# The gate table of the first layer: who builds its one-hot matrices

## The chip, the cores and the metric

The kernel runs on one core of a Trainium2 chip. The metric is the device time of one execution, in microseconds (us), as the median of several runs. Its engines are called as in the profile: PE (TensorE, with PEld for its weight loads), DVE (VectorE), ACT (ScalarE), POOL (GpSimd), SP (SyncE, which only issues DMAs here).

## What is computed

Two layers of token mixing (four head groups) and of a product-key expert network, PEER, on 256 latent and 256 context tokens. The part that matters here is the expert network of the first layer. Each token has 8 heads; each head picks 16 of 128 x 128 experts, and a gate for each:

```
best, sel = lax.top_k(cand, PEER_TOPK)
eidx = jnp.take_along_axis(cidx, sel, axis=-1)     # i * 128 + j
g = jax.nn.softmax(best, axis=-1)
act = jax.nn.gelu(jnp.einsum('td,thkd->thk', xb, u[eidx]))
return jnp.einsum('thk,thkd->td', (g * act), v[eidx])
```

So a token has 8 x 16 = 128 picks (i, j, gate). For the 256 latent tokens of the first layer the kernel does not gather rows of u and v. It runs all 16384 experts as dense matrix products and multiplies their activations by a table of gates G[j, i, token], which is zero wherever an expert was not picked. This table is what the changed stage builds.

## The kernel before

`phase_route` finds the picks and leaves three matrices iT, jT, gT, each 128 x 256: one column for each latent token, one partition for each of its 128 picks. `phase_dense` turns them into the table, `phase_mixed` uses it. `phase_dense` is called once, in the first layer. Each phase is a block of its own: all engines meet at a barrier before and after it, so no load of `phase_mixed` is issued while `phase_dense` runs, and the block ends only when its last store has landed.

For one token the table is one matrix product of two one-hot matrices, 128 picks x 128 keys each. `hot_j` holds 1 where the key equals j, `hot_i` holds the gate where the key equals i. PE multiplies them and leaves the token's 128 x 128 gates in PSUM.

The 256 tokens go through in 16 units of U = 16 tokens. `hot_i` and `hot_j` have two buffers each (r = unit mod 2), and so has PSUM (four of its eight banks per unit). For unit u:

- DVE (L1746) makes columns 0 to UJ - 1 of `hot_j`, UJ = 10 tokens, in a single comparison of `jT` and `iota`, both read from SBUF and broadcast: 128 x 1280 elements.
- DVE (L1750) then makes all 16 matrices of `hot_i`, one instruction each: 128 x 128 elements of `iota`, compared with the pointer scalar iT[:, token] and multiplied by the pointer scalar gT[:, token].
- ACT makes the other 6 tokens of `hot_j`: |iota - j| for each (L1783), then one relu(1 - x) over all six (L1786).
- PE (L1771) waits for all three (semaphores a, b, c), and for the PSUM buffer, and does 16 products. Each is in float32 and shows as two rows of the trace, so a unit is 32.
- ACT (L1800) copies the unit's PSUM, 128 x 2048, into `dense_stage`. ACT makes its columns of unit u + 1 before it copies unit u.
- SP (L1812) stores four units at once, 4 MB, to HBM.
- POOL has no work in this phase.

Before unit u, DVE waits until PE has done unit u - 2, which frees the buffer (`dve.wait_ge(g_mm, u - 1)`). The first eight units are written out, the other eight are the body of a register loop `Fori(1, 2)`, which runs once.

Of the kernel before, what the change touches and what calls it, by code (L numbers as in the profile page):

```python
# [33 lines left out]
ALU = mybir.AluOpType  # L34
ACT = mybir.ActivationFunctionType
AX = mybir.AxisListType.X

P = 128
# [46 lines left out]
NKEY = 128  # L85
TOPK = 16
GROWS = 4
TB = 64
# [34 lines left out]
def bc(ap, axis, n):  # L123

    ap = ap.unsqueeze(axis)
    shape = list(ap.shape)
    shape[axis] = n
    return ap.to_broadcast(shape)
# [13 lines left out]
def build(nc, d, out):  # L142
# [4 lines left out]
    def sem(name):  # L147
        layer_sems.append(nc.alloc_semaphore(name=name))
        return layer_sems[-1]
# [7 lines left out]
    def sb(st, name, shape, dt=F32):  # L157
        return st.enter_context(nc.sbuf_tensor(name, shape, dt))

    with ctx:  # L160
        ps = ctx.enter_context(nc.psum_tensor("ps", [P, 8, BANK], F32))
# [11 lines left out]
        iota = sb(ctx, "iota", [P, P])  # L173
        gates_dram = nc.dram_tensor("peer_gates", (T // TB, P, NKEY, TB), F32, kind="Internal").ap()
# [13 lines left out]
        class AdaPart:  # L188
# [53 lines left out]
            def columns(self, pe, i):  # L242

                pe.wait_ge(ada_row_ev, self.chunks0 + i + 1)
                for j in range(4):
                    o = 2 * (4 * i + j)
                    mm = nc.tensor.matmul(ps[:, self.banks[2], o:o + 2], self.row[:, i % 2, j * P:(j + 1) * P], sel[:],
                                          start=True, stop=True)
                mm.then_inc(ada_col_mm, 1)
# [1471 lines left out]
        def phase_dense(l, lo, iT, jT, gT):  # L1721


            n = T - lo
            U = 16
            UB = 8
            PB = TB // U
            UJ = 10
            a_done, b_done, g_mm, g_ev, neg_done, dist_done, c_done = (
                sem(f"dense_{x}{l}") for x in ("a", "b", "mm", "ev", "neg", "dist", "c"))  # L1730
            stored = [sem(f"dense_stored{l}_{r}") for r in range(2)]
            with ExitStack() as st:
                hot_i = sb(st, f"hot_i{l}", [P, 2, U, NKEY])
                hot_j = sb(st, f"hot_j{l}", [P, 2, U, NKEY])
                stage = sb(st, f"dense_stage{l}", [P, 2, NKEY, TB])
                njT = sb(st, f"dense_nj{l}", [P, n + U])
                with nc.Block() as block:
                    @block.vector
                    def _(dve):
                        def body(it, first):  # L1740
                            for q in range(UB):
                                u = UB * it + q
                                r = q % 2
                                if not (first and q < 2):
                                    dve.wait_ge(g_mm, u - 1)
                                nc.vector.tensor_tensor(hot_j[:, r, 0:UJ], bc(jT[:, bass.ds(u * U, UJ)], 2, NKEY),  # L1746
                                                        bc(iota[:], 1, UJ), ALU.is_equal).then_inc(b_done, 1)
                                for t in range(U):
                                    at = bass.ds(u * U + t, 1)
                                    last = nc.vector.tensor_scalar(hot_i[:, r, t], iota[:], iT[:, at], gT[:, at],  # L1750
                                                                   ALU.is_equal, ALU.mult)
                                last.then_inc(a_done, 1)
                        nc.vector.memset(njT[:, n:], 0.0).then_inc(neg_done, 1)
                        nc.vector.tensor_scalar(njT[:, 0:n], jT[:], -1.0, None, ALU.mult).then_inc(neg_done, 1)
                        body(0, True)
                        with dve.Fori(1, n // (U * UB)) as it:
                            body(it, False)

                    @block.tensor
                    def _(pe):  # L1760
                        def body(it, first):
                            for q in range(UB):
                                u = UB * it + q
                                r = q % 2
                                pe.wait_ge(b_done, u + 1)
                                pe.wait_ge(a_done, u + 1)
                                pe.wait_ge(c_done, u + 1)
                                if not (first and q < 2):
                                    pe.wait_ge(g_ev, u - 1)
                                for t in range(U):  # L1770
                                    mm = nc.tensor.matmul(ps[:, 4 * r + t // 4, (t % 4) * P:(t % 4 + 1) * P],  # L1771
                                                          hot_j[:, r, t], hot_i[:, r, t], start=True, stop=True)
                                mm.then_inc(g_mm, 1)
                        body(0, True)
                        with pe.Fori(1, n // (U * UB)) as it:
                            body(it, False)

                    @block.scalar
                    def _(act):
                        def columns(u, r):  # L1780

                            for t in range(UJ, U):
                                last = nc.scalar.activation(hot_j[:, r, t], iota[:], ACT.Abs, bias=njT[:, bass.ds(u * U + t, 1)])  # L1783
                            last.then_inc(dist_done, 1)
                            act.wait_ge(dist_done, u + 1)
                            nc.scalar.activation(hot_j[:, r, UJ:], hot_j[:, r, UJ:], ACT.Relu, scale=-1.0,  # L1786
                                                 bias=onecol[:]).then_inc(c_done, 1)

                        def body(it, first):
                            for q in range(UB):  # L1790
                                u = UB * it + q
                                if not (first and q == 0):
                                    act.wait_ge(g_mm, u)
                                columns(u + 1, (q + 1) % 2)
                                act.wait_ge(g_mm, u + 1)
                                if q % PB == 0 and not first:
                                    act.wait_ge(stored[q // PB], 16 * it)
                                got = ps[:, 4 * (q % 2):4 * (q % 2) + 4, :].rearrange("p b (t i) -> p i (b t)", i=NKEY)
                                o = (q % PB) * U
                                nc.scalar.activation(stage[:, q // PB, :, o:o + U], got, ACT.Copy).then_inc(g_ev, 1)  # L1800
                        act.wait_ge(neg_done, 2)
                        columns(0, 0)
                        body(0, True)
                        with act.Fori(1, n // (U * UB)) as it:
                            body(it, False)

                    @block.sync
                    def _(sp):
                        with sp.Fori(0, n // (U * UB)) as it:
                            for r in range(2):  # L1810
                                sp.wait_ge(g_ev, UB * it + PB * r + PB)
                                sp.dma_start(gates_dram[bass.ds(2 * it + r, 1)].rearrange("a p i t -> p (a i) t"),  # L1812
                                             stage[:, r]).then_inc(stored[r], 16)
                        for r in range(2):
                            sp.wait_ge(stored[r], 16 * (n // (U * UB)))


        def phase_stream(l, lo, hp, hT, q):
# [594 lines left out]
        for l in range(DEPTH):  # L2413
# [16 lines left out]
            with ExitStack() as st:  # L2430
# [3 lines left out]
                if last_layer:  # L2434
                    hp = [(CTX, T, *own)]
                    clear_layer_sems()
                    q = QueryWeights(st, l)
# [4 lines left out]
                else:  # L2442
                    eid, eidT = (sb(st, f"{x}{l}", [P, nt, PH * TOPK], U32) for x in ("eid", "eidT"))
                    gate = sb(st, f"gate{l}", [P, nt, PH * TOPK])
                    with ExitStack() as st1:
                        iT, jT, gT = (sb(st1, f"{x}T{l}", [P, T - CTX]) for x in "ijg")
                        with ExitStack() as st2:
                            hp = [(0, CTX, *(sb(st2, f"h2c_{x}{l}", [P, DC, CTX], F32R) for x in ("hi", "lo"))), (CTX, T, *own)]
                            q = QueryWeights(st2, l)
# [8 lines left out]
        with ExitStack() as st:  # L2458
            y = sb(st, "y", [P, DC, T])
            phase_norm("norm_final", d["final_norm_g"], None, None, CTX, y)  # L2460
            stored = sem("stored")
# [107 lines left out]
```

## Time and profile before

| | |
|---|---|
| median of 3 runs | 3184.79 us (3181.0 to 3188.43) |
| the profiled execution | 3183.49 us, its span 3181.7 us |
| busy, of the span | PE 80%, DVE 64%, ACT 34%, POOL 35% |
| `phase_dense`, DVE's first `hot_j` to the end of its last `hot_i` | 872.27 to 961.43 us, 89.2 us |
| mean granted TensorE clock | 0.888 of full speed |

A row of the timeline gives the start in us, the time from the first start to the last end, the engine, the line of the kernel, the operation, what it writes and reads, the shape, and how many instructions it merges; brackets give the idle time before and what ended it. Instructions of one engine overlap a little: the next starts before the last one's end, so the pace of a series is read from start to start. The columns of the other views stand with their rows below.

### The profile page before, as it was taken

Reading aid. Unit: us, or ns where it says so; the run is one execution under the profiler, and the core shown is the slowest. Engines: PE = TensorE matmul, PEld = TensorE weight load, DVE = VectorE, ACT = ScalarE, POOL = GpSimd, SP = SyncE. Lnnn points to the kernel's source line nnn. Section 1 sums busy time; section 2 is a strip of 40 time slices with the busy share of each in tenths; the row PEclk is TensorE's granted clock in tenths of the full one; section 3 lists DMA queues with packets and bytes.
Section 4 is the critical chain, followed back from the end, with each engine's and each line's share of the span. In section 5 each row is a group of like instructions: output and inputs, shape, how many; then the busy total and the mean of one; then the engine's idle time right before and its main releaser. Section 6 shows DMA issues by size and latency. Waiting matters only on the chain. (4 is left out here: it accounts for less than half of the span.)

```text
span 3181.7 us, 41584 instructions
## 1 busy us (share of the span) xinstructions
PE 2546.1 (80%) x15562; PEld 1903.4 (60%) x15562; DVE 2022.4 (64%) x4495; ACT 1084.4 (34%) x2179; POOL 1119.1 (35%) x1013
## 2 busy tenths in 40 slices
PE   5978699797376778878799999888877797777776
PEld 3778445595165777767777777577746553222222
DVE  3566435489995989887844333467543699845444
ACT  3422235321073333333333333342234443333332
POOL 1024100331005667556665555212302354433431
PEclk8985589897698989999999999988678899999999
DMA  5210141135238999999999999621002799999996
GB/s 208 74 30 1 62 159 42 53 113 180 106 152 325 405 407 404 363 401 385 402 406 406 405 406 406 263 87 43 9 1 85 303 391 422 421 421 422 421 422 258
DMA packets 211897, 816.93 MB, mean 257 GB/s; under 512 B 22681, under 2 KB 41689, under 8 KB 178033
## 3 DMA queue, kind: packets, MB, share of 16 engines
q0 software_dynamic: 110592, 536.92, 41.7%
q1 hardware_dynamic: 101104, 277.35, 23.4%
q8 instruction: 124, 2.03, 0.3%
q14 instruction: 77, 0.62, 0.1%
HBM read 796.37 MB, written 17.83 MB: 256 GB/s over the span
## 5 line engine op out<-in xcount | busy, mean ns | idle before, releaser
L1919 PE MATMUL ps<-pair_ring,pair_diag 128*128 128x512 f32 x1024 | 476.3, 610 | 144.8 <-ACT pair_diag L1993 142.2
L2103 DVE CUSTOM_DVE_ANT_0 pair_ring<-pair_ring,hT 128x1024 f32<-128x1024 f32 x256 | 312.9, 1222 | 206.7 <-DMA pair_ring<-in_uv_rows,eid 206.7
L1919 PEld LDWEIGHTS ps<-pair_ring,pair_diag 128*128 128x128 f32 x1024 | 187.1, 192 | 423.3 <-ACT pair_diag L1993 228.5
L1883 POOL DMA_INDIRECT pair_ring<-in_uv_rows,eid x256 | 268.2, 1048 | 391.9 <-PE ps L1919 364.0
L2251 POOL DMA_INDIRECT sparse_ring<-in_v_rows,eidT x256 | 279.5, 1092 | 298.4 <-PE ps L2300 226.9
L2251 POOL DMA_INDIRECT sparse_ring<-in_u_rows,eid x256 | 339.4, 1326 | 122.5 <-issue 68.1
L118 PE MATMUL ps<-h_hi,peer_uh 128*128 128x256 f32 x1024 | 310.1, 303 | 85.6 <-DVE peer_ul L2363 77.9
L2389 DVE CUSTOM_DVE_ANT_0 sparse_ring<-sparse_ring,hT 128x1024 f32<-128x1024 f32 x256 | 304.7, 1224 | 41.9 <-DMA sparse_ring<-in_u_rows,eid 35.7
L120 PE MATMUL ps<-h_hi,peer_ul 128*128 128x256 f32 x1024 | 299.2, 292 | 1.1 <-issue 0.9
L119 PE MATMUL ps<-h_lo,peer_uh 128*128 128x256 f32 x1024 | 299.4, 292 | 0.1
L118 PEld LDWEIGHTS ps<-h_hi,peer_uh 128*128 128x128 f32 x1024 | 206.0, 201 | 149.4 <-DVE peer_ul L2363 92.0
L118 PE MATMUL ps<-peer_wh,peer_vh 128*128 128x256 f32 x1024 | 291.3, 285 | 1.8 <-issue 1.7
L119 PE MATMUL ps<-peer_wl,peer_vh 128*128 128x256 f32 x1024 | 290.5, 284 | 0.4 <-issue 0.3
L120 PE MATMUL ps<-peer_wh,peer_vl 128*128 128x256 f32 x1024 | 290.1, 283 | 0.1
L2363 DVE TENSOR_TENSOR peer_ul<-peer_u,peer_uh 128x1024 fp32r<-128x1024 f32 x128 | 156.5, 1223 | 164.3 <-ACT peer_uh L2328 132.7
L2328 ACT ACTIVATE peer_uh<-peer_u 128x1024 fp32r<-128x1024 f32 x128 | 135.2, 1057 | 292.2 <-DMA peer_u<-in_uT 273.7
L120 PEld LDWEIGHTS ps<-h_hi,peer_ul 128*128 128x128 f32 x1024 | 206.2, 201 | 1.3 <-issue 1.3
L119 PEld LDWEIGHTS ps<-h_lo,peer_uh 128*128 128x128 f32 x1024 | 206.6, 202 | 0.2 <-issue 0.2
L118 PEld LDWEIGHTS ps<-peer_wh,peer_vh 128*128 128x128 f32 x1024 | 197.8, 193 | 2.6 <-issue 2.4
L119 PEld LDWEIGHTS ps<-peer_wl,peer_vh 128*128 128x128 f32 x1024 | 197.5, 193 | 2.1 <-issue 2.1
L120 PEld LDWEIGHTS ps<-peer_wh,peer_vl 128*128 128x128 f32 x1024 | 197.2, 193 | 0.8 <-issue 0.8
L2300 PE MATMUL ps<-sparse_ring,sparse_wdiag 128*32 128x512 f32 x1024 | 137.2, 653 | 67.2 <-DMA sparse_ring<-in_v_rows,eidT 66.2
(397 smaller groups left out, 5411.5 us busy)
## 6 DMA issues: line engine op xcount, KB each, us to landing
peer_u<-in_uT SPq DMA_DIRECT2D x128, 512.0 KB
peer_v<-in_v_rows SPq DMA_DIRECT2D x128, 512.0 KB
ada_slab<-in_ada_w SPq DMA_DIRECT2D x20, 2048.0 KB, 8.6
proj_slab<-in_w_fm SPq DMA_DIRECT2D x38, 512.0 KB
route_slab<-in_w_pq SPq DMA_DIRECT2D x32, 512.0 KB, 3.3
peer_gates<-dense_stage SPq DMA_DIRECT2D x4, 4096.0 KB, 13.1
peer_gates<-peer_gates SPq DMA_DIRECT2D x32, 512.0 KB
out_slab<-in_w_out SPq DMA_DIRECT2D x16, 512.0 KB, 3.7
```

What stands on the lines that cost most here:

```text
L118: nc.tensor.matmul(out, w[0], x[0], start=start, stop=False)
L119: nc.tensor.matmul(out, w[0], x[1], start=False, stop=False)
L120: return nc.tensor.matmul(out, w[1], x[0], start=False, stop=stop)
L1883: nc.gpsimd.indirect_dma_start(out=ring[:, s % R], out_offset=None, in_=d["uv_rows"], in_offset=bass.IndirectOffsetOnAxis(ap=eid[:, s:s + ...
L1919: mm = nc.tensor.matmul(ps[:, 4 + 2 * t + half, :], diag[:, s % DG, :], ring[:, s % R, D_MODEL + half * BANK:D_MODEL + (half + 1) * BANK], ...
L2103: nc.vector.tensor_tensor_reduce(out=row, in0=row, in1=hT[:, s // NS], scale=1.0, scalar=0.0, op0=ALU.mult, op1=ALU.add, accum_out=dots[:, ...
L2251: nc.gpsimd.indirect_dma_start(out=ring[:, s % R], out_offset=None, in_=rows, in_offset=bass.IndirectOffsetOnAxis(ap=at, axis=0)).then_inc ...
L2300: mm = nc.tensor.matmul(ps[32 * q:32 * (q + 1), 6 + half, :], wdiag[:, q, j, :], ring[:, s % R, half * BANK:(half + 1) * BANK], start=(j = ...
L2328: nc.scalar.activation(uh[:, e % 2], us[:, e % SW], ACT.Copy).then_inc(uhi, 1)
L2363: nc.vector.tensor_tensor(ul[:, e % 2], us[:, e % SW], f32(uh[:, e % 2]), ALU.subtract).then_inc(ulo, 1)
L2389: nc.vector.tensor_tensor_reduce(out=ring[:, s % R], in0=ring[:, s % R], in1=hT[:, t], scale=1.0, scalar=0.0, op0=ALU.mult, op1=ALU.add, a ...
```

## The change

Three things change in `phase_dense`, and nothing elsewhere:

1. `hot_i`: DVE makes the first UI = 10 of a unit's 16 matrices, POOL the last 6, by the same instruction (`nc.gpsimd.tensor_scalar`). POOL waits for the buffer as DVE does, and signals a semaphore of its own, `a_pool`, for which PE waits too.
2. `hot_j`: UJ goes from 10 to 12. DVE's comparison has 128 x 1536 elements; ACT makes four columns and not six.
3. The register loops of all engines are written out as 16 units.

```
-            UJ = 10
+            UJ = 12
+            UI = 10
...
+                        for u in range(NU16):
+                            r = u % 2
+                            if u >= 2:
+                                dve.wait_ge(g_mm, u - 1)
+                            nc.vector.tensor_tensor(hot_j[:, r, 0:UJ], bc(jT[:, u * U:u * U + UJ], 2, NKEY),
+                                                    bc(iota[:], 1, UJ), ALU.is_equal).then_inc(b_done, 1)
+                            for t in range(UI):
+                                at = slice(u * U + t, u * U + t + 1)
+                                last = nc.vector.tensor_scalar(hot_i[:, r, t], iota[:], iT[:, at], gT[:, at], ALU.is_equal, ALU.mult)
+                            last.then_inc(a_done, 1)
+
+                    @block.gpsimd
+                    def _(pool):
+                        for u in range(NU16):
+                            r = u % 2
+                            if u >= 2:
+                                pool.wait_ge(g_mm, u - 1)
+                            for t in range(UI, U):
+                                at = slice(u * U + t, u * U + t + 1)
+                                last = nc.gpsimd.tensor_scalar(hot_i[:, r, t], iota[:], iT[:, at], gT[:, at], ALU.is_equal, ALU.mult)
+                            last.then_inc(a_pool, 1)
...
+                            pe.wait_ge(b_done, u + 1)
+                            pe.wait_ge(a_done, u + 1)
+                            pe.wait_ge(a_pool, u + 1)
+                            pe.wait_ge(c_done, u + 1)
```

The order of DVE's instructions, from the start of the phase through unit 1 to the first wait for a buffer (`dense_mm0` is the semaphore g_mm). Before:

```order
L1754 TENSOR_SCALAR dense_nj<-jT 128x256
L1746 TENSOR_TENSOR hot_j<-jT,iota 128x1280
L1750 TENSOR_SCALAR hot_i<-iota,iT,gT 128x128 x16
L1746 TENSOR_TENSOR hot_j<-jT,iota 128x1280
L1750 TENSOR_SCALAR hot_i<-iota,iT,gT 128x128 x16
L1746 TENSOR_TENSOR hot_j<-jT,iota 128x1280 [waits dense_mm0]
```

In the changed kernel:

```order
L1743 TENSOR_SCALAR dense_nj<-jT 128x256
L1748 TENSOR_TENSOR hot_j<-jT,iota 128x1536
L1752 TENSOR_SCALAR hot_i<-iota,iT,gT 128x128 x10
L1748 TENSOR_TENSOR hot_j<-jT,iota 128x1536
L1752 TENSOR_SCALAR hot_i<-iota,iT,gT 128x128 x10
L1748 TENSOR_TENSOR hot_j<-jT,iota 128x1536 [waits dense_mm0]
```

Six instructions of a unit have left DVE's queue, and the comparison is wider; the wait stands at the same place.

The order of POOL's instructions at the same place, as a piece of the difference (the rows without a sign are in both). POOL goes from the routing phase into the new work; units 0 and 1 wait for nothing, and are the first twelve:

```order
 L1638 TENSOR_TENSOR route_wl<-route_slab,route_wh 128x1024 [waits query_hi0] x14
 L1541 UNCONDITIONAL_BRANCH
+L1755 UNCONDITIONAL_BRANCH [waits barrier_Pool_Activation_PE_DVE_SP_gather]
+L1763 TENSOR_SCALAR hot_i<-iota,iT,gT 128x128 x12
+L1763 TENSOR_SCALAR hot_i<-iota,iT,gT 128x128 [waits dense_mm0]
+L1763 TENSOR_SCALAR hot_i<-iota,iT,gT 128x128 x5
```

The last two rows repeat for each of units 2 to 15. Where POOL had nothing, it now has 96 instructions in the phase, and PE waits for each sixth.

## Rows read from the trace of the kernel before

**Rows 1.** Timeline of DVE from 922.5 us, in the middle of the phase.

```profile
922.80 1.48 DVE L1746 TENSOR_TENSOR hot_j<-jT,iota 128x1280 f32<-128x1280 f32 x1
924.20 4.19 DVE L1750 TENSOR_SCALAR hot_i<-iota,iT,gT 128x128 f32<-128x128 f32 x16
928.31 1.48 DVE L1746 TENSOR_TENSOR hot_j<-jT,iota 128x1280 f32<-128x1280 f32 x1
```

**Rows 2.** Timelines of PE and of ACT in the same stretch.

```profile
922.99 3.81 PE L1771 MATMUL ps<-hot_i,hot_j 128*128 128x128 f32 x32 [1.69 <-issue]
...
923.10 1.85 ACT L1783 ACTIVATE hot_j<-iota,dense_nj 128x128 f32<-128x128 f32 x6
924.99 0.93 ACT L1786 ACTIVATE hot_j<-hot_j,onecol 128x768 f32<-128x768 f32 x1
926.83 1.88 ACT L1800 ACTIVATE dense_stage<-ps 128x2048 f32<-128x2048 f32 x1 [0.91 <-PE ps L1771]
```

**Rows 3.** Timeline of all engines, start and end of the phase.

```profile
872.27 1.49 DVE L1746 TENSOR_TENSOR hot_j<-jT,iota 128x1280 f32<-128x1280 f32 x1
...
877.96 7.28 PE L1771 MATMUL ps<-hot_i,hot_j 128*128 128x128 f32 x42 [7.14 <-ACT hot_j L1786]
...
884.17 1.49 DVE L1746 TENSOR_TENSOR hot_j<-jT,iota 128x1280 f32<-128x1280 f32 x1 [0.80 <-PE ps L1771]
...
957.24 4.18 DVE L1750 TENSOR_SCALAR hot_i<-iota,iT,gT 128x128 f32<-128x128 f32 x16
...
965.36 1.88 ACT L1800 ACTIVATE dense_stage<-ps 128x2048 f32<-128x2048 f32 x1 [0.91 <-PE ps L1771]
980.25 0.34 SPq L2229 DMA_DIRECT2D peer_u<-in_uT  x1
```

**Rows 4.** Single lines: count, duration in ns (min/median/max), first and last start.

```profile
L1783 ACT ACTIVATE hot_j<-iota,dense_nj x102: 385/390/401, 872.4 to 963.1; 128x128 f32<-128x128 f32 x102
...
L2363 DVE TENSOR_TENSOR peer_ul<-peer_u,peer_uh x128: 1209/1224/1300, 985.9 to 2015.1; 128x1024 fp32r<-128x1024 f32 x128
```

**Rows 5.** Busy us by stretch (PE, PEld, DVE, ACT, POOL), then granted PE clock.

```profile
878.00:884.00 6.00, 6.00 (x33) 6.00 (x34) 5.37 (x17) 0.00 (x0) 0.00 (x0) 0.59 0.00 0
```

**Rows 6.** Lines of POOL as in rows 4; the last has count, busy us, mean ns.

```profile
L630 POOL TENSOR_SCALAR mix<-mix,mod x12: 1012/1064/1599, 47.7 to 2075.9; 128x256 f32<-128x256 f32 x12
...
L811 POOL TENSOR_TENSOR scan_exk<-cum x28: 393/590/791, 236.2 to 2262.4; 128x256 f32<-128x256 f32 x14, 128x128 f32<-128x128 f32 x14
...
L630 POOL TENSOR_SCALAR mix<-mix,mod 128x256 f32<-128x256 f32 x12 | 13.9, 1171 | 92.2 <-ACT h_hi L597 92.2
```

**Rows 7.** Timelines of POOL and of DVE around 52 to 55 us.

```profile
51.59 2.11 POOL L630 TENSOR_SCALAR mix<-mix,mod 128x256 f32<-128x256 f32 x2
...
52.44 1.09 DVE L734 SCALAR_TENSOR_TENSOR mix<-xT,norm_mix_amp,proj_tslab 128x256 f32<-128x256 f32 x2
...
55.26 0.87 DVE L719 SCALAR_TENSOR_TENSOR h_lo<-mix,mod,h_hi 128x256 fp32r<-128x256 f32 x2
```

**Rows 8.** Timelines of DVE and of POOL from 631 us.

```profile
631.11 0.28 DVE L440 CAST h2c_hi<-h 128x256 fp32r<-128x256 f32 x1
631.31 0.83 DVE L440 CAST h_hi<-h 128x256 fp32r<-128x256 f32 x1
...
631.26 0.73 POOL L457 TENSOR_TENSOR h2c_lo<-h,h2c_hi 128x256 fp32r<-128x256 f32 x1 [0.76 <-DVE h_hi L440]
```

**Rows 9.** Timelines of POOL and of DVE from 224 us.

```profile
224.13 3.96 POOL L807 TENSOR_TENSOR scan_exq<-cum 128x256 f32<-128x256 f32 x1 [13.09 <-DVE scan_lk L857]
228.05 0.61 POOL L808 TENSOR_TENSOR scan_exk<-cum 128x256 f32<-128x256 f32 x1
...
226.92 0.68 DVE L870 TENSOR_TENSOR mix<-fm 128x512 f32<-128x512 f32 x1
```

**Rows 10.** Single lines of DVE, one and two pointer scalars, columns as in rows 4.

```profile
L1323 DVE TENSOR_SCALAR diag<-ident,rinv x48: 285/286/290, 423.4 to 2400.7; 128x128 f32<-128x128 f32 x48
...
L1325 DVE TENSOR_SCALAR diag<-ident,rinv,nlam x24: 345/346/348, 482.9 to 2401.5; 128x128 f32<-128x128 f32 x24
```

More of the change, by code:

```diff
@@ L1727, in phase_dense @@
             PB = TB // U
-            UJ = 10
-            a_done, b_done, g_mm, g_ev, neg_done, dist_done, c_done = (
-                sem(f"dense_{x}{l}") for x in ("a", "b", "mm", "ev", "neg", "dist", "c"))
+            UJ = 12
+            UI = 10
+            NU16 = n // U
+            a_done, a_pool, b_done, g_mm, g_ev, neg_done, dist_done, c_done = (
+                sem(f"dense_{x}{l}") for x in ("a", "a_pool", "b", "mm", "ev", "neg", "dist", "c"))
             stored = [sem(f"dense_stored{l}_{r}") for r in range(2)]
@@ L1739, in _ @@
                     def _(dve):
[L1740 to L1752, printed above, removed]
@@ L1753, in _ @@
                         nc.vector.memset(njT[:, n:], 0.0).then_inc(neg_done, 1)
                         nc.vector.tensor_scalar(njT[:, 0:n], jT[:], -1.0, None, ALU.mult).then_inc(neg_done, 1)
-                        body(0, True)
-                        with dve.Fori(1, n // (U * UB)) as it:
-                            body(it, False)
+                        for u in range(NU16):
[8 more added lines that the diff above has]
+                            last.then_inc(a_done, 1)
@@ L1759, in _ @@
                     @block.tensor
                     def _(pe):
[L1761 to L1773, printed above, removed]
@@ L1774, in _ @@
-                        body(0, True)
-                        with pe.Fori(1, n // (U * UB)) as it:
-                            body(it, False)
+                        for u in range(NU16):
+                            r = u % 2
+                            pe.wait_ge(b_done, u + 1)
+                            pe.wait_ge(a_done, u + 1)
+                            pe.wait_ge(a_pool, u + 1)
+                            pe.wait_ge(c_done, u + 1)
+                            if u >= 2:
+                                pe.wait_ge(g_ev, u - 1)
+                            for t in range(U):
+                                mm = nc.tensor.matmul(ps[:, 4 * r + t // 4, (t % 4) * P:(t % 4 + 1) * P],
+                                                      hot_j[:, r, t], hot_i[:, r, t], start=True, stop=True)
+                            mm.then_inc(g_mm, 1)
@@ L1778, in _, with columns @@
                     @block.scalar
                     def _(act):
-                        def columns(u, r):
+                        def columns(u):
+                            r = u % 2
                             for t in range(UJ, U):
-                                last = nc.scalar.activation(hot_j[:, r, t], iota[:], ACT.Abs, bias=njT[:, bass.ds(u * U + t, 1)])
+                                last = nc.scalar.activation(hot_j[:, r, t], iota[:], ACT.Abs, bias=njT[:, u * U + t:u * U + t + 1])
@@ L1787, in columns @@
                                                  bias=onecol[:]).then_inc(c_done, 1)
[L1789 to L1792, printed above, removed]
-                                    act.wait_ge(g_mm, u)
[L1794 to L1805, printed above, removed]
+                        act.wait_ge(neg_done, 2)
+                        columns(0)
+                        for u in range(NU16):
+                            if u + 1 < NU16:
+                                if u >= 1:
+                                    act.wait_ge(g_mm, u)
+                                columns(u + 1)
+                            act.wait_ge(g_mm, u + 1)
+                            b = u // PB
+                            if u % PB == 0 and b >= 2:
+                                act.wait_ge(stored[b % 2], 16 * (b // 2))
+                            got = ps[:, 4 * (u % 2):4 * (u % 2) + 4, :].rearrange("p b (t i) -> p i (b t)", i=NKEY)
+                            o = (u % PB) * U
+                            nc.scalar.activation(stage[:, b % 2, :, o:o + U], got, ACT.Copy).then_inc(g_ev, 1)
@@ L1807, in _ @@
                     @block.sync
                     def _(sp):
[L1809 to L1813, printed above, removed]
+                        for b in range(n // TB):
+                            sp.wait_ge(g_ev, PB * (b + 1))
+                            sp.dma_start(gates_dram[b:b + 1].rearrange("a p i t -> p (a i) t"), stage[:, b % 2]).then_inc(stored[b % 2], 16)
@@ L1814, in _ @@
                         for r in range(2):
-                            sp.wait_ge(stored[r], 16 * (n // (U * UB)))
+                            sp.wait_ge(stored[r], 16 * (n // TB // 2))
         def phase_stream(l, lo, hp, hT, q):
```

## The prediction

> **What bounds the kernel now.** The change touches one stage of 3%, so I read that stage and not the shares of the span. I took the timeline of the middle of the phase first, engine by engine. DVE has no gap: a unit begins at 922.80 and the next at 928.31, so a unit costs 5.51 us [rows 1]. 1.40 us of it is the comparison (from its start to the start of what follows), 4.11 us the sixteen `hot_i`, 0.257 us each. PE works 3.81 us of a unit and idles 1.69; ACT is busy 1.85 + 0.93 + 1.88 = 4.66 us [rows 2]. The waits say the same: DVE waits for PE once, 0.80 us before unit 2 [rows 3], while ACT waits 0.91 us for PE in each unit [rows 2]. DVE is the bound, and PE's idle time is time in which it waits for DVE.
>
> Next I asked whether the stage's time reaches the end of the kernel. The last copy to the stage buffer ends at 967.24, and the first load of the next phase is issued at 980.25, after the store has landed and the engines have met [rows 3]. Nothing of the next phase starts early, so each microsecond that the last unit moves goes whole to the end. From DVE's first comparison to the end of its last `hot_i` it is 961.42 - 872.27 = 89.2 us [rows 3]: sixteen units of 5.51 and 1 us of wait and start. This is the number that the change moves.
>
> **The change, part by part.**
>
> *DVE.* It loses six `hot_i`: 6 x 0.257 = 1.54 us of a unit. Its comparison grows from 1280 to 1536 elements. 1280 take 1.48 us [rows 1], 1024 take 1.22 [rows 4], so 256 more cost 0.26. A unit of DVE becomes 5.51 - 1.54 + 0.26 = 4.23 us, if nothing disturbs it.
>
> *ACT.* It loses two |iota - j| of six (1.85 us) and a third of the relu. Four cost some 1.26 us; the relu over 512 columns lies between 0.39 us at 128 [rows 4] and 0.93 at 768 [rows 2], in proportion 0.72. With the copy ACT has 3.86 us. ACT was not the bound at 4.66 and is not now; this move costs or gives something only through DVE's 0.26.
>
> *PE.* Same products, one more wait. 3.81 us at full clock. At the start it is slower: the first unit's products run from 877.96 until they release DVE at 884.17, 6.2 us [rows 3], with a granted clock of 0.59 [rows 5], between the levels 1.2 and 2.4 GHz; PE had idled before. That binds only where a unit is under 6.2 us.
>
> *The loops.* The loop body ran once, so writing it out removes a branch or two on each engine. DVE's `hot_i` have the same pace in the first eight units and in the loop: 16 in 4.19 us at 924.20 and in 4.18 at 957.24 [rows 1, 3]. I cost it at nothing.
>
> *POOL.* This is the term that decides. Six instructions of 128 x 128 with two pointer scalars and two operations; the trace has none. Nearest is L630, the same kind, with one pointer scalar and 256 columns: median 1064 ns, and a pair takes 2.11 us, 1.055 each [rows 6, 7]. How much of that goes with the columns? While such an instruction runs, a pair of DVE's takes 1.09 us instead of 0.87 [rows 7]: DVE is held 0.22 us, for 256 columns. I take that as the part that goes with the columns, and the rest of the 1.06 us as a fixed part, during which DVE runs on. Half the columns save 0.11: 0.945 us. The second pointer scalar costs 0.06 us on DVE (346 against 286 ns) [rows 10], and I put as much on POOL: **1.0 us**. Bounds: below, the fastest two-tensor instruction of POOL at 128 columns, 0.39 us; above, the mean of the twelve of L630, 1.17 us [rows 6], with 0.06 for the pointer 1.23. I stay near L630 as it is the same kind of instruction. Six then take 6.0 us (2.4 to 7.4). The point from which POOL decides is low: 5.51 / 6 = 0.92 us each.
>
> The Trainium skill ("GPSIMD Engine Reference", 4.1 Engine selection) says of elementwise work on GpSimd that one-input operations are roughly at line rate. By that (an estimate from its 1.2 GHz clock: 128 columns in 0.11 us, and a dispatch) POOL would be hidden, and the sum would be that of the faster rival below. The row of 1064 ns for 256 columns [rows 6] speaks against it, and I go by the row.
>
> *POOL against DVE.* The two disturb each other, in both directions. A cast of DVE, 0.28 us alone, takes 0.83 when it starts 0.05 us after an instruction of POOL [rows 8]. And POOL's instruction at 224.13 takes 3.96 us instead of 0.61: it finishes only 0.5 us after the last of a burst of DVE's two-input instructions, the one that ends at 227.60 [rows 9]. So DVE's wide comparison (two inputs, 1.66 us here) can hold POOL once a unit by 0 to 1.66 us. A fixed part of an instruction of POOL can pass meanwhile; half of that part is 0.4 us, and less is lost for some phases of the two, so I take 0.9. In return POOL holds DVE by 6 x 0.11 = 0.66 us a unit: DVE's 4.23 become 4.9.
>
> *Sum.* DVE 4.9, ACT 3.9, PE 3.8, POOL 6.0 + 0.9 = 6.9 us. With two buffers POOL works back to back, since PE's unit is done 3.9 us after POOL's and the next-but-one buffer is free by then. PE waits for `a_pool` in every unit, and DVE, done early, waits for PE. Sixteen units of 6.9 are 110.4 us in place of 89.2: +21.2. The profiled execution has 3183.49 us, so 3204.7; the median of the runs shown is 1.3 above it. **Forecast: 3206 us.** This case's own range: units of 5.9 to 7.4 + 1.66 = 9.0 us, +5 to +55, that is 3190 to 3240.
>
> **The rivals.**
>
> *Faster: DVE stays the bound.* If POOL's instruction costs 0.39 to 0.65 us, POOL's six and one hold stay below DVE's 4.9. Then 16 x 4.9 = 78.4 us, and the first two units of PE at the low clock add 2 x (6.2 - 4.9) = 2.6: 81.0, or 8 us less than now, 3177 us. If the holds come to nothing too, 16 x 4.23 and 3.9 for the two units are 71.6: 17.6 less, 3167. For it: 590 ns is the median of POOL's two-tensor instructions [rows 6]. Against: L630 never took less than 1012.
>
> *No change: a draw.* POOL's instruction at 0.70 to 0.83 us, or holds that rarely meet, give units of 5.2 to 5.9 us: within 6.4 us of now, 3185. It would mean that L630's fixed part is shorter without DVE beside it. That the written-out loops are all that counts would end here too.
>
> *Much slower: the two exclude each other whole.* If a running instruction of POOL holds DVE for its full length, as in [rows 8], and DVE holds POOL for all of its own, a unit is 4.23 + 6.0 = 10.2 us: 164 in place of 89.2, +74, 3259 us. The 0.22 us of [rows 7] speaks against it for this kind of instruction. The Trainium skill ("SBUF — State Buffer", Who interferes with whom) says that VectorE and GpSimd share a pair of ports, and that whoever issues first gets the shared pair "for the whole instruction"; by that rule this rival would be the forecast, at 3259 us; [rows 7] show less.
>
> **How the numbers follow.** A change under 0.2% (6.4 us) can't be told from none in this kernel. POOL as the bound 0.57; DVE as the bound 0.22; the draw 0.16; exclusion 0.05. That gives faster 0.22, same 0.16, slower 0.62. The sign hangs on one price, POOL's instruction: 0.92 us with no hold at all, about 0.8 with the hold that I expect. The range goes from 3174 to 3240: up to the upper bound of the forecast's case, down into the faster one; it leaves out exclusion, and the part of the faster rival with hardly any holds (0.08).
>
> **What would show it.** Right: L1763 on POOL at about 1 us with no gap between units, one of six longer; DVE's `hot_j` (L1748) waiting for PE by some 2 us in each unit; PE's wait for `hot_i` of L1763; unit starts 6.9 us apart. DVE's `hot_i` above 0.257 us in pace shows the holds. The forecast is wrong if POOL idles before its first instruction of each unit, waiting for PE: then its six fit, and DVE or PE sets the pace. Outside this phase all stages should keep their times.

## The result, and the profile after

The changed kernel takes **3208.71 us** (median of 4 runs, 3203.66 to 3210.25), in place of 3184.05 with the runs of before repeated beside it: a ratio of 1.0072, 95% interval 1.0058 to 1.0086. It is slower, by about 25 us; the forecast was 3206.

| | before | after |
|---|---|---|
| span of the profiled execution | 3181.7 us | 3207.2 us |
| DVE's first `hot_j` | 872.27 | 873.50 |
| first `hot_j` to the end of the last `hot_i` of either engine | 89.1 us | 111.3 us |
| first load of the next phase | 980.25 | 1003.82 |
| one unit, later part of the phase | 5.51 us | 6.88 us |
| POOL, instructions and busy time in the phase | none | 96, 104.5 us |

The phase gives 22.1 us of the 25.5 between the two spans. 1.2 us were there when it began, and some 2 us came after it; both lie in code that the change doesn't touch, and the runs of one kernel differ by more (from 3203.66 to 3210.25 here).

Timelines of the changed kernel, each of one engine, in the middle of the phase: DVE, then PE, then POOL (cut at different places, so the counts go with the cut).

```profile
921.14 1.75 DVE L1748 TENSOR_TENSOR hot_j<-jT,iota 128x1536 f32<-128x1536 f32 x1
922.81 2.80 DVE L1752 TENSOR_SCALAR hot_i<-iota,iT,gT 128x128 f32<-128x128 f32 x10
930.66 1.76 DVE L1748 TENSOR_TENSOR hot_j<-jT,iota 128x1536 f32<-128x1536 f32 x1 [5.05 <-PE ps L1777]
...
935.01 1.74 DVE L1748 TENSOR_TENSOR hot_j<-jT,iota 128x1536 f32<-128x1536 f32 x1
...
925.28 8.92 PE L1777 MATMUL ps<-hot_i,hot_j 128*128 128x128 f32 x64 [4.95 <-POOL hot_i L1763]
...
930.73 2.45 POOL L1763 TENSOR_SCALAR hot_i<-iota,iT,gT 128x128 f32<-128x128 f32 x1 [0.97 <-PE ps L1777]
...
934.84 2.42 POOL L1763 TENSOR_SCALAR hot_i<-iota,iT,gT 128x128 f32<-128x128 f32 x1
...
939.74 3.88 POOL L1763 TENSOR_SCALAR hot_i<-iota,iT,gT 128x128 f32<-128x128 f32 x5
944.50 2.45 POOL L1763 TENSOR_SCALAR hot_i<-iota,iT,gT 128x128 f32<-128x128 f32 x1 [0.88 <-PE ps L1777]
```

Beside [rows 1, 2], DVE has lost its place as the bound: it works in pairs of units, two comparisons 4.35 us apart, and then waits 5.05 us for PE. PE waits 4.95 us for POOL, and does two units in one go. POOL is busy from 930.73 to 943.62 and idle for 0.88 us: 12 of its instructions in 13.77 us, two units. At the end of a pair, with DVE idle, five in a row take 3.88 us, a pace of 0.773 us. Two of the twelve take much longer, and both meet a comparison. The first of the pair takes 2.45 us: it starts 0.07 us after DVE's comparison, and ends 0.8 us after the comparison has given way to the `hot_i`. The fourth starts at 934.84, 0.17 us before the second comparison, and takes 2.42 us; the comparison takes its 1.74 us all the same. I call this lengthening the hold.

The waits of the whole phase (total, times, longest):

```profile
PE ps L1777 <- POOL hot_i L1763: 44.5, 8, 9.9
DVE hot_j L1748 <- PE ps L1777: 36.6, 7, 6.2
...
POOL hot_i L1763 <- PE ps L1777: 8.1, 7, 2.1
```

Lines of the changed kernel (count, ns min/median/max), and two stretches (busy us of PE, PEld, DVE, ACT, POOL, then the granted clock):

```profile
L1748 DVE TENSOR_TENSOR hot_j<-jT,iota x16: 1744/1746/1759, 873.5 to 976.2; 128x1536 f32<-128x1536 f32 x16
...
L1752 DVE TENSOR_SCALAR hot_i<-iota,iT,gT x160: 330/386/430, 875.2 to 980.3; 128x128 f32<-128x128 f32 x160
...
L1763 POOL TENSOR_SCALAR hot_i<-iota,iT,gT x96: 783/834/2497, 873.3 to 984.0; 128x128 f32<-128x128 f32 x96
...
925.30:930.60 5.30, 5.30 (x34) 5.30 (x35) 0.32 (x2) 0.00 (x0) 4.46 (x6) 0.70 0.00 0
930.70:939.00 8.30, 3.50 (x32) 3.31 (x30) 8.30 (x21) 7.37 (x12) 8.27 (x7) 0.99 0.30 126
```

The first unit of a pair is multiplied after PE has idled for 5 us, with a granted clock of 0.70 between the levels 1.2 and 2.4 GHz, and takes 5.4 us (925.28 to 930.66) where 3.8 would do. This is what POOL then waits for: the first unit of the next pair needs this one's buffer. POOL's own work on a pair is done before that: in the next pair at 943.62, where PE's first unit is done at 944.43.

### The profile page after: what moved, and what is told of

The parts are those of the page before. It is cut to its first block and busy times, and to the rows that moved or that the text cites. A ratio compares the mean times of both kernels' runs of the same rounds, so it can differ in the third digit from the quotient of the medians.

```text
span 3207.2 us, 41519 instructions
## 1 busy us (share of the span) xinstructions
PE 2549.8 (80%) x15562; PEld 1907.5 (59%) x15562; DVE 2003.9 (62%) x4399; ACT 1067.8 (33%) x2140; POOL 1232.3 (38%) x1109
## 5 line engine op out<-in xcount | busy, mean ns | idle before, releaser
L2249 POOL DMA_INDIRECT sparse_ring<-in_u_rows,eid x256 | 346.5, 1354 | 119.3 <-issue 68.1
```

The costliest lines, as they stand in the source:

```text
L2249: nc.gpsimd.indirect_dma_start(out=ring[:, s % R], out_offset=None, in_=rows, in_offset=bass.IndirectOffsetOnAxis(ap=at, axis=0)).then_inc ...
```

## The experiments

Three things could carry the 22 us: the price of POOL's instruction, the hold by DVE's comparison, and the clock. The experiments take them apart. In the ratios "before" is the kernel before, run beside them; the phase is measured as in the table above, in the one execution that was profiled, while the times are medians of 4 to 11 runs.

**The loops alone.**

```
-            UI = 10
+            UI = 16
-            UJ = 12
+            UJ = 10
...
-                            pe.wait_ge(a_pool, u + 1)
```

with POOL's block taken out.

> Only the loops are written out: UJ = 10, all sixteen hot_i on VectorE, none on GpSimd. My theory (all of the 25 us comes from GpSimd's part): units of 5.51 us as before, the phase from the first hot_j to the end of the last hot_i 89.2 us, the time within 6 us of before, 3184. Rival (the straight code costs something of its own, in fetching): units longer than 5.51, the time up to 10 us above before.

3183.52 us, ratio 0.9998 (0.9985 to 1.0011), phase 88.8 us. DVE's timeline in it:

```profile
922.08 1.47 DVE L1748 TENSOR_TENSOR hot_j<-jT,iota 128x1280 f32<-128x1280 f32 x1
923.49 4.18 DVE L1752 TENSOR_SCALAR hot_i<-iota,iT,gT 128x128 f32<-128x128 f32 x16
927.59 1.47 DVE L1748 TENSOR_TENSOR hot_j<-jT,iota 128x1280 f32<-128x1280 f32 x1
```

A unit of 5.51 us, as in [rows 1]. The loops are worth nothing here.

**The two columns back on ACT.** `-UJ = 12`, `+UJ = 10` in the changed kernel.

> As the changed kernel, with the two columns of hot_j back on ScalarE (UJ = 10). Theory (VectorE's two-input comparison holds GpSimd for its whole length, once a unit, and GpSimd is the bound): a comparison shorter by 0.26 us shortens every unit by 0.26 us, 6.88 to 6.62, the phase 111.3 to about 107 us, the time about 4 us under the changed kernel, 3204. Rival (VectorE has slack, so its 0.26 us is hidden; the hold does not go with the comparison's length): the phase stays at 111 us, the time at 3208.

3205.48 us, ratio 1.0053 (1.0036 to 1.0069), phase 109.2 us: 2.1 us less than the changed kernel, half of what I expected. (The ratios of the two, 1.0053 and 1.0072, have intervals that overlap, so it is the phase that tells them apart.) Its waits:

```profile
PE ps L1777 <- POOL hot_i L1763: 40.3, 8, 9.4
DVE hot_j L1748 <- PE ps L1777: 38.8, 7, 6.3
...
POOL hot_i L1763 <- PE ps L1777: 10.2, 7, 2.2
```

The longest instruction of POOL fell from 2497 to 2232 ns, and its busy time by 3.9 us (104.5 to 100.6), as the hold's theory says. But POOL's wait for PE grew from 8.1 to 10.2 us: half of the gain went there. Moving the columns to DVE was a small loss of its own, through the hold and not through DVE's time.

**No two-input comparison.**

```
-                            nc.vector.tensor_tensor(hot_j[:, r, 0:UJ], bc(jT[:, u * U:u * U + UJ], 2, NKEY),
-                                                    bc(iota[:], 1, UJ), ALU.is_equal).then_inc(b_done, 1)
+                            for t in range(UJ):
+                                at = slice(u * U + t, u * U + t + 1)
+                                last = nc.vector.tensor_scalar(hot_j[:, r, t], iota[:], jT[:, at], None, ALU.is_equal)
+                            last.then_inc(b_done, 1)
```

> As the changed kernel, but VectorE makes its twelve columns of hot_j with twelve one-input instructions with a pointer scalar, instead of one comparison of two inputs. VectorE gets more work: 12 x 0.20 = 2.4 us in place of 1.67. Theory (the comparison holds GpSimd): without it GpSimd's six cost about 0.83 to 0.85 us each, 5.1 us, VectorE needs 2.4 + 2.57 + 0.3 = 5.3 us, a unit is 5.3 to 5.5 us and the phase about 87 us: the time 3182, 26 us under the changed kernel. Rival (the long first instruction of GpSimd in each unit has another cause, such as starting after a wait): the phase stays at 111 us or above, the time 3208 or more.

3180.92 us, ratio 0.9987 (0.9977 to 0.9998), phase 86.2 us. DVE got more work, and the phase became 25.1 us shorter. Its lines, PE's longest wait for DVE or POOL, and a stretch:

```profile
L1750 DVE TENSOR_SCALAR hot_j<-iota,jT x192: 269/275/393, 871.0 to 954.0; 128x128 f32<-128x128 f32 x192
...
L1765 POOL TENSOR_SCALAR hot_i<-iota,iT,gT x96: 834/845/1156, 870.8 to 956.3; 128x128 f32<-128x128 f32 x96
...
PE ps L1779 <- DVE hot_i L1754: 26.7, 14, 7.0
...
900.00:940.00 40.00, 29.13 (x248) 27.97 (x246) 40.00 (x166) 27.42 (x45) 40.00 (x46) 1.00 0.50 211
```

No instruction of POOL is above 1.16 us now, and the one that PE sees come last is DVE's. POOL has no gap either, so the two are level. DVE does not stop POOL with its one-input instructions, but it delays it: the 96 have a mean of 0.90 us, from 0.84 beside the `hot_i` to as much as 1.16 beside the `hot_j`, in place of the 0.79 of POOL alone. The 25.1 us are not the hold's alone: the pairs are gone too, and the clock is granted in full, so this run takes away the hold and POOL's wait for a slow PE together. That these instructions of DVE disturb POOL far less than the comparison is measured; which port each of them uses is not.

**TensorE kept busy.**

```
+                            if u >= 2:
+                                pe.wait_ge(g_ev, u - 1)
+                                for t in range(8):
+                                    nc.tensor.matmul(ps[:, 4 * r, 0:P], ident[:], ident[:], start=True, stop=True)
                             pe.wait_ge(b_done, u + 1)
...
                             pe.wait_ge(c_done, u + 1)
-                            if u >= 2:
-                                pe.wait_ge(g_ev, u - 1)
```

> As the changed kernel, with eight products of the identity by itself before each unit from the third on, into the PSUM bank that the unit then overwrites; TensorE waits for that bank first and for the one-hots after. Theory (in every second unit the products run at the lower clock after 5 us of idling, 5.4 us instead of 3.8, and GpSimd then waits 0.97 us for their end): with the clock kept up GpSimd does not wait, the phase falls from 111.3 to about 103.5 us, the time to 3201. Rival (that wait is not the clock's): the phase stays at 111 us, or grows where the filler gets in the way of the second of two units.

3203.2 us, ratio 1.0053 (1.0036 to 1.007), phase 105.3 us: 6.0 us less than the changed kernel, 7.8 expected. A stretch of it, the same stretch of the changed kernel, and POOL's wait in the filler run:

```profile
900.00:964.00 64.00, 55.72 (x480) 54.11 (x479) 45.85 (x114) 38.36 (x64) 64.00 (x61) 1.00 0.43 182
```

```profile
900.00:964.00 64.00, 41.90 (x308) 41.06 (x306) 41.14 (x100) 35.45 (x57) 58.79 (x54) 0.88 0.31 132
```

```profile
POOL hot_i L1763 <- PE ps L1779: 2.9, 2, 1.8
```

The clock is granted in full, POOL has no gap in the 64 us, and from the seventh unit on DVE's comparisons come evenly, 6.4 us apart: 6 x 0.80 and one hold of 1.6. The first units still came in pairs, which is probably most of what is missing.

**GpSimd's price.** In the changed kernel, POOL only compares (for six of sixteen tokens the gate is left out):

```
-                                last = nc.gpsimd.tensor_scalar(hot_i[:, r, t], iota[:], iT[:, at], gT[:, at], ALU.is_equal, ALU.mult)
+                                last = nc.gpsimd.tensor_scalar(hot_i[:, r, t], iota[:], iT[:, at], None, ALU.is_equal)
```

> As the changed kernel, but GpSimd's instructions only compare: one pointer scalar and one operation. It leaves out the multiplication by the gate for six of sixteen tokens. Undisturbed they took 0.773 us with two. If the forecast's reading of the nearest row was right but for the second pointer's price (0.06 us), they now take about 0.71 us, and the 1.05 us of 256 columns means 0.34 us for 128 columns more. If the fixed part is smaller and the columns cost more than the 0.11 us read from VectorE's delay, the same 0.34 us shows it, or more where the second scalar is dear: at 0.60 us, 0.45. A unit should shorten by six times the difference, 0.4 us at 0.71 (the phase by 6 us) and 1.0 us at 0.60 (16 us).

3201.32 us, ratio 1.0045 (1.0028 to 1.0061), phase 103.1 us. POOL's line and timeline, PE's and DVE's rows for the second half of a pair, and two stretches:

```profile
L1763 POOL TENSOR_SCALAR hot_i<-iota,iT x96: 591/597/2188, 872.9 to 975.6; 128x128 f32<-128x128 f32 x96
```

```profile
925.16 10.11 POOL L1763 TENSOR_SCALAR hot_i<-iota,iT 128x128 f32<-128x128 f32 x12 [3.49 <-PE ps L1777]
...
927.31 2.33 POOL L1763 TENSOR_SCALAR hot_i<-iota,iT 128x128 f32<-128x128 f32 x4
...
938.79 10.11 POOL L1763 TENSOR_SCALAR hot_i<-iota,iT 128x128 f32<-128x128 f32 x12 [3.52 <-PE ps L1777]
...
932.02 10.24 PE L1777 MATMUL ps<-hot_i,hot_j 128*128 128x128 f32 x64 [3.38 <-POOL hot_i L1763]
...
938.73 1.76 DVE L1748 TENSOR_TENSOR hot_j<-jT,iota 128x1536 f32<-128x1536 f32 x1 [4.51 <-PE ps L1777]
```

```profile
924.50:930.00 5.50, 4.14 (x38) 3.95 (x36) 4.89 (x12) 4.86 (x7) 4.83 (x6) 1.00 0.00 0
...
935.00:939.00 4.00, 4.00 (x25) 4.00 (x25) 0.27 (x1) 0.27 (x1) 0.48 (x2) 0.62 1.22 518
```

Four in 2.33 us with a last one of 0.597 are a pace of 0.578 us, so the second scalar and the second operation cost 0.195 us. L630, with one scalar and 256 columns, never took under 1012 ns [rows 6], these never under 591: by that 128 columns are worth 0.42 us, an estimate, since L630 adds where these compare. The time is where the expectation failed: 12 instructions fell from 12.9 to 10.1 us, and a pair of units still takes 13.63 (925.16 to 938.79) after 13.77. POOL idles 3.5 us of it, waiting for the first unit of the pair on PE, which runs from 932.02 to 938.73 at the low clock. The bound had moved to PE, whose granted clock is low after it has idled for 3.4 us.

**The same, with TensorE kept busy** (four products of the identity before each unit):

> The last kernel (GpSimd only compares; it leaves out the gate for six of sixteen tokens) with four products of the identity before each unit from the third on, as in the filler run, where they were eight. There GpSimd's price had fallen by a quarter and two units still took 13.6 us, with a granted clock of 0.62 while the first of the two was multiplied. Theory (TensorE's clock after its idle time is what holds the pace there): with TensorE kept busy a unit costs what GpSimd costs, 6 x 0.577 + 1.6 = 5.1 us, the phase falls from 103 to 83 to 86 us and the time by 17 to 20 us, to 3183. Rival (the pace of pairs comes from the buffers and the comparisons, not from the clock): 6.5 us or more a unit, the phase at 100 us or above.

3188.79 us, ratio 1.0014 (1.0003 to 1.0024), phase 86.5 us, 16.6 us less than without the filler. Stretch and POOL's timeline:

```profile
900.00:930.00 30.00, 25.19 (x221) 24.90 (x222) 24.95 (x61) 20.82 (x35) 27.96 (x34) 1.00 0.58 245
```

```profile
927.05 8.40 POOL L1763 TENSOR_SCALAR hot_i<-iota,iT 128x128 f32<-128x128 f32 x9 [0.68 <-PE ps L1779]
```

A pair takes 10.8 us, 5.4 a unit, where 5.1 were expected. Both holds of a pair fall into its first unit; POOL's six of the second are then done in 3.5 us, before PE's 3.8 at full clock are, and POOL waits 0.68 us a pair. So the clock was the bound of the run before: four useless products a unit took 16.6 us off its phase. The times moved less, by 12.5 us, or some 10 by the two ratios, and this one lies above before although its phase is the shorter one. The profiled execution took 3183.7 us, 5 under the median; what the rest is, no run shows.

**Other shares.** The prices say that four on POOL fit. Three runs in the changed kernel with other UI and UJ.

> As the changed kernel, with UI = 12 and UJ = 10: GpSimd makes four of sixteen, ScalarE keeps its six columns. By the prices measured so far: GpSimd 4 x 0.82 + a hold of 1.35 = 4.6 us a unit, VectorE 1.40 + 12 x 0.257 + 4 x 0.05 = 4.7, ScalarE 4.5 to 4.7, TensorE 3.8 and slower in the first units. Units of 4.7 us, the phase 77 to 80 us in place of 89.2: the time 3174 to 3177, about 10 us under before. Rival (with VectorE, ScalarE and GpSimd within 0.2 us of each other, waits between them add up): units of 5.0 us or more, the gain under 6 us.

> As the one before, with UI = 13: GpSimd makes three. GpSimd 3 x 0.82 + 1.35 = 3.8 us and idle, VectorE 1.40 + 13 x 0.257 + 3 x 0.05 = 4.9 us and the bound: units of 4.9 us, the phase 79 to 82 us, the time 3176 to 3179. If waits between the engines are what costs at UI = 12, this one is the faster of the two; if not, it is slower by 0.2 us a unit, 3 us.

> As UI = 12, with UJ = 11: one column goes from ScalarE to VectorE. ScalarE falls to 4.2 us, VectorE rises to 4.8, GpSimd's hold to 1.48 and its unit to 4.8. If VectorE and GpSimd set the pace, units of 4.8 us and the time 2 us above UJ = 10; rival (at UJ = 10 ScalarE's 4.5 to 4.7 us is what binds): faster than UJ = 10 or the same.

| UI, UJ | median | ratio (95%) | phase | unit |
|---|---|---|---|---|
| 12, 10 | 3172.97 us | 0.9962 (0.9948 to 0.9976) | 76.6 us | 4.64 us |
| 13, 10 | 3177.59 us | 0.9978 (0.9970 to 0.9987) | 78.9 us | 4.83 us |
| 12, 11 | 3173.69 us | 0.9963 (0.9950 to 0.9976) | 78.5 us | 4.78 us |

The phases order the three as the prices do; the medians can't tell 12, 10 from 12, 11. The timeline of the first, and a stretch of it:

```profile
921.72 1.48 DVE L1748 TENSOR_TENSOR hot_j<-jT,iota 128x1280 f32<-128x1280 f32 x1
...
922.02 3.81 PE L1777 MATMUL ps<-hot_i,hot_j 128*128 128x128 f32 x32 [0.83 <-DVE hot_i L1752]
...
923.12 3.41 DVE L1752 TENSOR_SCALAR hot_i<-iota,iT,gT 128x128 f32<-128x128 f32 x12
...
926.36 1.48 DVE L1748 TENSOR_TENSOR hot_j<-jT,iota 128x1280 f32<-128x1280 f32 x1
...
900.00:940.00 40.00, 33.11 (x280) 31.63 (x278) 40.00 (x115) 39.27 (x72) 40.00 (x36) 1.00 0.56 237
```

DVE has no gap, PE idles 0.83 us and keeps its clock. POOL has no gap either, so its four have no room left. With UI = 12 and UJ = 10 the kernel is 12 us faster than before and 36 faster than the changed one, by two numbers: the hold and the price are there still, but four of sixteen just fit beside DVE's twelve.

## Why the prediction was right, and which terms were off

**The forecast's case came.** POOL became the bound, PE waits for its semaphore, the phase grew by 22.1 us (21.2 in the sum), and 6.88 us a unit stand where 6.9 were forecast. That the two agree so closely is luck: three terms were mis-sized, and they cancel.

- *POOL's instruction, 1.0 us.* Measured 0.773 alone and 0.83 beside DVE's `hot_i`. The step that failed is "I take that as the part that goes with the columns": DVE's delay of 0.22 us was read as the cost of 256 columns to POOL, so halving them saved only 0.11. By the run without the gates they save about 0.42. The second pointer scalar, with the second operation, costs 0.20 and not DVE's 0.06. Six: 4.8 us, not 6.0.
- *The hold, 0.9 us.* Measured 1.6 a unit, nearly the whole length of the comparison (2.45 us in place of 0.83). "Half of that part is 0.4 us, and less is lost for some phases" assumed that the fixed part of POOL's instruction could pass under the comparison; it doesn't. [rows 9] had shown it: there POOL finished only after the last instruction of the burst.
- *"With two buffers POOL works back to back, since PE's unit is done 3.9 us after POOL's ..."* The first unit of a pair is done 5.4 us after, since PE has idled and its clock is low. 0.9 to 1.0 us of idling a pair of units, 8.1 us in the phase. The forecast's sum had nothing for this: the prediction saw the low clock at the start alone, where it "binds only where a unit is under 6.2 us".
- With the sizes measured, a unit is six instructions, one hold and half of a pair's idling: 6 x 0.80 + 1.6 + 0.48 = 6.9 us, where the forecast had 6.0 + 0.9 + 0.

**What held.** DVE's comparison has 1746 ns (1.74 = 1.48 + 0.26 predicted). POOL's holds on DVE were put at 0.11 each, and are some 0.05: ten `hot_i` and the comparison take 4.35 us with two or three of them in place of 4.23. ACT needs 1.26 + 0.72 + 1.88, as forecast. The loops cost nothing. Nothing outside the phase moved beyond a run's scatter.

**The signs that the prediction named.** DVE's `hot_j` was to wait some 2 us in each unit; it waits 5.05 us in each second one. That the forecast is "wrong if POOL idles before its first instruction of each unit" was too sharp: it idles before each second unit, for PE, and is the bound all the same. An engine can wait a little each round, and the round be set by the time it takes plus the answer it waits for.

**The rivals.** The faster one hung on a price of 0.39 to 0.65 us. The run without the gates has 0.577, and was still slower than before: with a hold of 1.6 and a clock that falls, a cheap instruction doesn't suffice. The draw's prices (0.70 to 0.83) are what was measured; by the sum, with the hold as forecast, it would have been the result. Mutual exclusion for whole instructions holds in one direction only, for these two kinds: DVE's comparison stops POOL for nearly its full length, while each of POOL's one-input instructions delays DVE's `hot_i` by some 0.05 us, and the comparison not at all (all sixteen take 1744 to 1759 ns). The Trainium skill ("SBUF — State Buffer", Who interferes with whom) has a two-input instruction of VectorE contend with GpSimd's reads, as seen here; that whoever issues first gets the pair "for the whole instruction" does not fit. POOL's instruction at 934.84 started before the comparison, and it was the one that was held.

## What to carry to other kernels

Before an instruction goes to GpSimd, price it by a row of the same kind and width, and add the length of a wide two-input VectorE instruction that runs beside it. Not every two-input instruction costs that much: VectorE's of 256 columns ran beside GpSimd's pair in [rows 7], and the pair took 2.11 us, where the shortest of its kind takes 1.01 us each [rows 6]. A share that fits by the instruction's own price (6 x 0.83 = 5.0 us under 5.51) can lose by the hold. Try two or three splits: four of sixteen gained 12 us where six lost 25. And when an engine before TensorE gets slower, price the products at the low clock too, since TensorE will idle before them.

## What the runs showed that I had not expected

- With two buffers and a late engine the units fall into pairs: PE waits 4.95 us, does two units at once, and DVE fills both buffers at once. Two comparisons in 4.35 us then meet POOL, and both holds fall into the first unit of the pair: POOL's second unit is done in 4.7 us (six from 938.92 to 943.62).
- TensorE's clock can become the bound of a stage in which TensorE has slack. In the run without the gates it was granted in full in one stretch and 0.62 in the next. Eight useless products a unit in the changed kernel, and four in the run without the gates, kept it at 1.00 in the stretches shown, 64 and 30 us long, and shortened the phase by 6 and 17 us.
- On GpSimd a second pointer scalar with its operation costs 0.195 us on 128 columns, 0.06 on VectorE [rows 10].
